# Both output projections of each layer as three products of rounded parts, with their weights split by ScalarE and GpSimd

## The reference, cut to what matters

```python
h = h + hybrid_mixer(rmsnorm(h, norm_mix[i]), ...)   # ends in concatenate([o_a, o_b, o_c, o_d]) @ w_out
h = h + cross_attn(rmsnorm(h, norm_xa[i]), mem, ...) # ends in o @ wo
h = h + swiglu(...)       # layer 0;  moe_swiglu(...) with 8 experts, top 2, in layer 1
```

## Time and profile before

| | us |
|---|---|
| median of 3 runs | 1512.05 (1511.49 to 1512.98) |
| the profiled execution | 1512.51 |
| its span in the trace | 1510.7 |
| PE busy | 1450.5 |
| DVE busy | 1086.0 |
| ACT busy | 914.1 |
| POOL busy | 51.8 |

### The profile page before, as it was taken

One profiled execution on the slowest core, in us unless ns is written; L12 is line 12 of the kernel. 1 busy time (PEld: TensorE's weight loads), 2 busy tenths in 40 slices (PEclk: granted clock), 3 DMA queues, 4 the chain that ended last, 5 costly groups with the idle time before them and its releaser, 6 DMA issues.

```text
span 1510.7 us, 19223 instructions
## 1 busy us (share of the span) xinstructions
PE 1450.5 (96%) x7312; PEld 1143.1 (76%) x7312; DVE 1086.0 (72%) x1116; ACT 914.1 (61%) x965; POOL 51.8 (3%) x64
## 2 busy tenths in 40 slices
PE   7999999999999999999999999999999999899997
PEld 5776679999877666788888777777777677677675
DVE  1615255555452526988798799899899898998996
ACT  2222243344322224777777688788887797887885
POOL 0230000000014000000000000000000000000000
PEclk9999999999999999999999999999999999999999
DMA  9522523542553055799899899999999999999991
GB/s 320 182 104 77 203 82 128 208 168 85 189 202 109 29 203 201 261 366 371 305 367 365 332 399 415 409 415 413 412 416 410 415 417 406 419 417 407 413 419 59
DMA packets 120581, 435.04 MB, mean 288 GB/s; under 512 B 5694, under 2 KB 30420, under 8 KB 113364
## 3 DMA queue, kind: packets, MB, share of 16 engines
q1 hardware_dynamic: 120340, 433.83, 74.6%
q0 software_dynamic: 192, 0.53, 0.1%
HBM read 433.28 MB, written 1.05 MB: 288 GB/s over the span
## 4 chain that ended last, share of the span: by engine, by line
PE 66%; DVE 17%; issue 12%; ACT 4%; DMA 0%; SPq 0%; DVEq 0%; ACTq 0%
PE bank L1902 23%; PE bank L1474 12%; DVE ring_lo L1380 12%; PE bank L1451 8%; PE bank L1456 6%; PE bank L1736 4%; PE bank L1928 3%; ACT w_hi L865 2%; PE bank L1848 2%; PE bank L1910 1%; DVE h L1217 1%; PE bank L1440 1%; PE bank L1778 1%; PE bank L1631 1%; PE bank L1430 1%
## 5 line engine op out<-in xcount | busy, mean ns | idle before, releaser
L1380 DVE TENSOR_TENSOR ring_lo<-ring,w_hi 128x2048 fp32r<-128x2048 f32 (+1 forms) x352 | 731.7, 2121 | 74.2 <-ACT w_hi L865 73.5
L865 ACT ACTIVATE w_hi<-ring 128x2048 fp32r<-128x2048 f32 (+1 forms) x352 | 610.3, 1777 | 138.1 <-PE bank L1902 138.0
L1902 PE MATMUL bank<-w_hi,xg 128*128 128x512 f32 x1120 | 408.5, 395 | 5.2 <-DVE ring_lo L1380 4.0
L1902 PE MATMUL bank<-ring_lo,xg 128*128 128x512 f32 x896 | 360.3, 402 | 19.4 <-DVE ring_lo L1380 17.3
L1902 PEld LDWEIGHTS bank<-w_hi,xg 128*128 128x128 f32 x1120 | 211.5, 189 | 51.1 <-DVE ring_lo L1380 4.4
L1902 PEld LDWEIGHTS bank<-ring_lo,xg 128*128 128x128 f32 x896 | 168.4, 188 | 76.1 <-DVE ring_lo L1380 41.6
L1902 PE MATMUL bank<-ring_lo,at_hi 128*128 128x512 f32 x400 | 162.3, 406 | 5.0 <-DVE at_hi L1363 5.0
L1902 PE MATMUL bank<-w_hi,at_hi 128*128 128x512 f32 x400 | 157.5, 394 | 0.5 <-DVE at_lo L1365 0.5
L1160 DVE TENSOR_TENSOR wf_lo<-ring,wf_hi 128x1024 fp32r<-128x1024 f32 x66 | 80.6, 1223 | 60.0 <-ACT wf_hi L743 60.0
L743 ACT ACTIVATE wf_hi<-ring 128x1024 fp32r<-128x1024 f32 x66 | 69.6, 1058 | 70.4 <-PE bank L1474 68.8
L1902 PEld LDWEIGHTS bank<-ring_lo,at_hi 128*128 128x128 f32 x400 | 75.1, 188 | 41.6 <-DVE ring_lo L1380 22.2
(11 more groups left out here) (337 smaller groups left out, 1635.3 us busy)
## 6 DMA issues: line engine op xcount, KB each, us to landing
ring<-in_moe_w SPq DMA_DIRECT2D x168, 2048.0 KB, 11.6
ring<-in_ffn_w SPq DMA_DIRECT2D x18, 1536.0 KB, 6.7
ring<-in_w_in SPq DMA_DIRECT2D x6, 2048.0 KB, 15.2
ring<-in_w_out SPq DMA_DIRECT2D x8, 1024.0 KB, 5.0
ring<-in_ffn_w SPq DMA_DIRECT2D x3, 2048.0 KB, 7.8
ring<-in_w_in SPq DMA_DIRECT2D x4, 1024.0 KB, 15.0
ring<-in_xa_wkv SPq DMA_DIRECT2D x2, 2048.0 KB, 14.8
ring<-in_w_in SPq DMA_DIRECT2D x2, 1184.0 KB, 7.3
```

Of the source, the lines that this page charges most:

```text
L865: act.activation(w_hi[:, i % NB, 0:cols.stop - cols.start], ring[:, slot_of(u), cols], ACT.Copy)\
L1380: dve.tensor_tensor(ring_lo[slot_of(u)][:, cols], ring[:, slot_of(u), cols], w_hi[:, i % NB, 0:cols.stop - cols.start], sub).then_inc(S["l ...
L1902: ins = mm(dst[:, :], st_, mv, start=opens, stop=closes, skip_group_check=small)
```

## The change

Both output projections become three products of rounded parts each. Their slots hold 2048 elements in a half of a slot of 4096, so the other half is free.

- ACT rounds the f32 weights of the slot into its upper half (`row_hi`), once for each of the five slots of a layer (`ROWS`: the four of `w_out`, and U_WO). These five instructions stand behind the copies kT, kdr, bu, uv0 and the copy of group 3.
- POOL writes the rest over the f32 weights in the lower half (`row_lo`), two before its wait for `bu`, three behind `pool_out`. It counts them up in `wkv_scaled`, six a layer with the scaling of U_WKV.
- DVE splits the activations: y is first scaled into `pw1`, then rounded to `mix_hi` and its rest put in `mix_lo`; groups 0, 2 (rows 0:2, 4:6) and the output of the cross-attention get a copy and a subtraction each, group 3 (rounded by ACT) a subtraction. `mix_hi` has the place of `mixT`, `mix_lo` the upper half of slot U_WQ.
- PE runs `times_rows`, with 12 products a token tile and group, and waits for POOL's count before each.

The diff, without the lines that only rename:

```diff
+        mix_hi = nc.alloc_sbuf_tensor_at("mix_hi", [P, KT, SEQ], F32R, offset=base, align_bytes=32)
+        mix_lo = ring_lo[U_WQ][:, 2048:4096].rearrange("p (k c) -> p k c", k=KT)
+        xo_hi, xo_lo = mix_hi[:, 0:2, :], mix_hi[:, 2:4, :]
...
+        ROWS = tuple(U_WOUT + n for n in range(4)) + (U_WO,)
...
+            return ring_lo[ROWS[n]][:, 2048:4096]
...
+            return ring_lo[ROWS[n]][:, 0:2048]
...
                 i.then_inc(S["wkv_scaled"], 1)
 
+                def rows_split(n):
+
+                    gp.wait_ge(S["bias_row"], hi_of_rows(layer, n))
+                    gp.tensor_tensor(row_lo(n), ring[:, ROWS[n], 0:2048], row_hi(n), ALU.subtract)\
+                      .then_inc(S["wkv_scaled"], 1)
+                for n in range(2):
+                    rows_split(n)
                 gp.wait_ge(g_ev["bu"], L1)
...
                 gp.wait_ge(S["pool_out"], L1)
+                for n in range(2, len(ROWS)):
+                    rows_split(n)
...
+                def rows_split(n):
+
+                    act.wait_ge(arrived[ROWS[n]], (layer * (16 * LAYER_TURNS) + 32))
+                    act.activation(row_hi(n), ring[:, ROWS[n], 0:2048], ACT.Copy).then_inc(S["bias_row"], 1)
                 out_of("k", kT[:, :, :], v3(ps[4], 0, 512, 2))
+                rows_split(0)
                 act.wait_ge(S["kd_ps"], L1)
                 act.activation(kdr, v3(ps[2], 0, 256, 2), ACT.Copy).then_inc(S["kdr_done"], 1)
+                rows_split(1)
                 out_of("bu", bu[:, :, PAD:PAD + SEQ], v3(ps[6], 0, 512, 2))
+                rows_split(2)
                 out_of("uv0", uvg[:, 0, :], ps[7][:, :], ACT.Gelu_apprx_tanh)
+                rows_split(3)
                 out_of("uv1", uvg[:, 1, :], ps[4][:, :], ACT.Gelu_apprx_tanh)
...
+                act.activation(mix_hi[:, 6:8, :], v3(ps[7], 0, 512, 2), ACT.Copy).then_inc(S["mt_a"], 1)
+                rows_split(4)
...
-                    i = dve.tensor_scalar(mixT[:, 2 + m, :], ps[5][:, 256 * m:256 * m + 256],
+                    i = dve.tensor_scalar(pw1[:, m, PAD:PAD + SEQ], ps[5][:, 256 * m:256 * m + 256],
                                           pcol[:, R_PB + m:R_PB + m + 1], pcol[:, R_PS + m:R_PS + m + 1], add, mult)
-                i.then_inc(g_ev["y"], 1)
+                link(i)
+                link(dve.tensor_copy(mix_hi[:, 2:4, :], pw1[:, :, PAD:PAD + SEQ]))
+                dve.tensor_tensor(mix_lo[:, 2:4, :], pw1[:, :, PAD:PAD + SEQ], mix_hi[:, 2:4, :], sub)\
+                   .then_inc(g_ev["y"], 1)
...
-                dve.tensor_copy(mixT[:, 0:2, :], v3(ps[4], 0, 512, 2)).then_inc(S["mt_v"], 1)
+                link(dve.tensor_copy(mix_hi[:, 0:2, :], v3(ps[4], 0, 512, 2)))
+                dve.tensor_tensor(mix_lo[:, 0:2, :], v3(ps[4], 0, 512, 2), mix_hi[:, 0:2, :], sub).then_inc(S["mt_v"], 1)
+                dve.wait_ge(S["mt_a"], L1)
+                dve.tensor_tensor(mix_lo[:, 6:8, :], v3(ps[7], 0, 512, 2), mix_hi[:, 6:8, :], sub).then_inc(S["mt_v"], 1)
                 dve.wait_ge(S["mto_ps"], L1)
-                dve.tensor_copy(mixT[:, 4:6, :], v3(ps[5], 0, 512, 2)).then_inc(S["mt_v"], 1)
+                link(dve.tensor_copy(mix_hi[:, 4:6, :], v3(ps[5], 0, 512, 2)))
+                dve.tensor_tensor(mix_lo[:, 4:6, :], v3(ps[5], 0, 512, 2), mix_hi[:, 4:6, :], sub).then_inc(S["mt_v"], 1)
...
-                dve.tensor_copy(oxT[:, :, :], v3(ps[1], 0, 512, 2)).then_inc(S["xo_done"], 1)
+                link(dve.tensor_copy(xo_hi, v3(ps[1], 0, 512, 2)))
+                dve.tensor_tensor(xo_lo, v3(ps[1], 0, 512, 2), xo_hi, sub).then_inc(S["xo_done"], 1)
...
+                def times_rows(bank, xh, xl, n, opens, closes):
+
+                    pe.wait_ge(S["wkv_scaled"], lo_of_rows(layer, n))
+                    wh, wl = v3(row_hi(n), 0, 2048, 2), v3(row_lo(n), 0, 2048, 2)
+                    for half in range(2):
+                        cs = slice(512 * half, 512 * half + 512)
+                        for k in range(2):
+                            for x, y in ((xh, wh), (xh, wl), (xl, wh)):
+                                i = mm(ps[bank + half][:, :], x[:, k, :], y[:, k, cs],
+                                       start=opens and k == 0 and x is xh and y is wh,
+                                       stop=closes and k == 1 and x is xl)
+                    return i
```

More of the change, by code:

```diff
@@ L201, in build @@
         base = nc.sbuf_base
+        assert base % 32 == 0
         xnT = sb("xnT", [P, KT, SEQ])
-        mixT = xnT
+        mix_hi = nc.alloc_sbuf_tensor_at("mix_hi", [P, KT, SEQ], F32R, offset=base, align_bytes=32)
+        mix_lo = ring_lo[U_WQ][:, 2048:4096].rearrange("p (k c) -> p k c", k=KT)
+        xo_hi, xo_lo = mix_hi[:, 0:2, :], mix_hi[:, 2:4, :]
         qidx = sb("qidx", [P, 1024])
@@ L322, in build @@
         vn = uvg[:, :, 256:512]
-        oxT = kT
         f_sil = v3(uvg[:, 1, :], 0, 512, 2)
@@ L407, in ffn_buf, with row_hi, row_lo, hi_of_rows @@
             return bufs[:, (i + NB - FFN_EARLY) % NB, :]
+        ROWS = tuple(U_WOUT + n for n in range(4)) + (U_WO,)
+        def row_hi(n):
+            return ring_lo[ROWS[n]][:, 2048:4096]
+        def row_lo(n):
+            return ring_lo[ROWS[n]][:, 0:2048]
+        def hi_of_rows(layer, n):
+            return 1 + len(ROWS) * layer + (n + 1)
+        def lo_of_rows(layer, n):
+            return (len(ROWS) + 1) * layer + (n + 2)
         def as_piece(w, buf):
@@ L716, in _ @@
                 act.wait_ge(S["mt_ps"], L1)
-                act.activation(mixT[:, 6:8, :], v3(ps[7], 0, 512, 2), ACT.Copy).then_inc(S["mt_a"], 1)
+                act.activation(mix_hi[:, 6:8, :], v3(ps[7], 0, 512, 2), ACT.Copy).then_inc(S["mt_a"], 1)
+                rows_split(4)
                 norm(1, R_XA)
@@ L1647, in _ @@
                 pe.wait_ge(arrived[U_WKV], landed[1])
-                pe.wait_ge(S["wkv_scaled"], L1)
+                pe.wait_ge(S["wkv_scaled"], lo_of_rows(layer, 0) - 1)
                 pe.wait_ge(g_ev["uv0"], L1)
@@ L1724, in _ @@
                         transpose_rows(5, oc).then_inc(S["mto_ps"], 1)
-                        pe.wait_ge(S["mt_v"], first)
+                        pe.wait_ge(S["mt_v"], 3 * layer + 1)
                     elif m == 3:
-                        pe.wait_ge(S["mt_a"], L1)
+                        pe.wait_ge(S["mt_v"], 3 * layer + 2)
                     else:
-                        pe.wait_ge(S["mt_v"], second)
+                        pe.wait_ge(S["mt_v"], 3 * layer + 3)
                     s = U_WOUT + i4
                     pe.wait_ge(arrived[s], landed[1])
-                    w = v3(ring[:, s, :], 0, 2048, 2)
                     for t in range(TT):
[L1734 to L1738, removed]
+                        i = times_rows(2 * t, mix_hi[:, 2 * m:2 * m + 2, P * t:P * t + P],
+                                       mix_lo[:, 2 * m:2 * m + 2, P * t:P * t + P], i4, i4 == 0, i4 == 3)
                         if i4 == 3 and t == 0:
@@ L1773, in _ @@
                 pe.wait_ge(arrived[U_WO], landed[1])
-                w = v3(ring[:, U_WO, :], 0, 2048, 2)
                 for t in range(TT):
[L1776 to L1779, removed]
+                    i = times_rows(4 + 2 * t, xo_hi[:, :, P * t:P * t + P], xo_lo[:, :, P * t:P * t + P], 4, True, True)
                     if t == 0:
```

## The result

| | us |
|---|---|
| before, median of 6 | 1511.88 (1510.96 to 1514.05) |
| changed, median of 6 | 1517.83 (1516.69 to 1518.67) |
| ratio | 1.0038, 95% interval 1.0028 to 1.0048 |
| profiled execution of the changed kernel | 1516.69, span 1514.9 |

The change makes the kernel 5.9 us slower, where 4 us less were forecast; the time lies outside the range. (The lines of `kernel.py` move: L1736 and L1778 are now L1774, L1045 is L1084, L912 is L951, L1071 is L1110, L1456 is L1503, POOL's subtraction is L588.)

The account below looks back on a forecast made before the run. PE, busy 96% of the span, was taken as the bound, its chain running through the two projections. Gains of 6.85 less 1.65 for splits and 3.1 for DVE's hold left 2.1 us a layer: 1508.3, about 1508.0 as median, range 1500.9 to 1511.5.

Parts of the forecast that it names:

- PE's new idle times: PE's added waits from the change, 1 to 3 us, were to leave its granted clock as it was.
- The row it rested on: Trace row cited for the unchanged clock: a stretch of 12 us with PE busy for 6.77 had 1.00.
- Products: Both output projections as three rounded products at 0.231 us each: 5.35 and 1.5 less, together 6.85 us a layer.
- Group y 1.0: Before the output projection, DVE's copy and subtraction for the first group delay PE's start: cost 1.0 us.
- xo 0.65: Before the cross-attention's projection, DVE's subtraction and its wait come on top: cost 0.65 us.
- ScalarE's roundings: Five roundings of 1.93 us on ACT, placed before waits of 4.97 to 8.24 us: cost nothing.
- GpSimd's subtraction 4.2: POOL's subtraction of 128x2048 takes 4.2 us, ends 3.0 and 6.2, four times the row at 128x512 being 4.16.
- The hold: POOL's third and fourth subtractions block DVE's bias_and_choice and small tensor_scalar: DVE 4.5 us late, 3.1 reaching the projection's start.
- Rival 1: DVE's small tensor_scalar is hardly held, lateness stays within the slack of 1.43 us, 5.2 a layer stands: 1501.9; chance 0.28.
- Rival 2: POOL's subtraction takes 6.2 us, DVE is 9.6 late, net 3.0 lost a layer: 1518; chance 0.08.
- point of decision: Threshold for a slower kernel: a loss of 5.2 us, DVE 6.6 late, a POOL instruction of about 5.2.
- Rival 3: Projections' products stay above 0.231 us, nothing gained at 0.287: 1512 to 1518; chance 0.04.

Follow-up runs that it names:

- the filled kernel: Changed kernel with six products of zero use added on PE where it waits, around the second tile's attention; 1511.0 us, ratio to before 0.9987.
- three ways of avoiding them: Changed kernel with GpSimd's subtractions moved away from DVE's SBUF work (1505.3 us), without the small tensor_scalar (1503.7), or with each subtraction cut into four (1504.7).
- the moved kernel: Changed kernel with ScalarE's roundings earlier, three of GpSimd's subtractions before bu's pooling and two behind group y; 1505.3 us, ratio 0.9956.
- the scalars from SBUF: Changed kernel with the small tensor_scalar of the gated MLP's variance taking its two scalars from SBUF, not as immediates; 1519.0 us, ratio 1.0045.
- the splits alone: Kernel before plus only ScalarE's five roundings and GpSimd's five subtractions a layer, projections still f32 products; 1527.9 us, ratio 1.0109.
- DVE late by itself: Kernel before with four reductions of 1.22 us put into DVE's queue behind bias_and_choice, DVE 5.0 us late; 1527.4 us, ratio 1.0101.
- quartered: Changed kernel with each of GpSimd's subtractions cut into four of 128x512; 1504.7 us, ratio 0.9955.

## Why the prediction was wrong

**The step that failed** is the last sentence of its sum: "PE's new idle times, 1 to 3 us, leave the clock as it is". The waits came as forecast, 1.1 and 1.7 us, and behind them the clock fell to 1.2 GHz and cost 4.85 us in layer 0 and 2.77 in layer 1. Filling the waits gave it back, and DVE's lateness alone, with nothing of the change, brought it about again (1527.4 us).

The row it rested on was read wrongly. The earlier trace rows shows 1.00 over 12 us with PE busy for 6.77, but it ends at 608.0, and PE came back from a wait of 3.99 us at 607.72. The next stretch of the same kernel, and its first product:

```profile
608.00:610.00 2.00, 2.00 (x6) 1.54 (x6) 2.00 (x4) 0.00 (x0) 0.00 (x0) 0.50 0.00 0
```

```profile
607.72 0.57 PE L1902 MATMUL bank<-w_hi,xg 128*128 128x512 f32 x1 [3.99 <-DVE ring_lo L1380]
```

The kernel before shows the fall; it stands in the records of the products behind a wait, not in the stretch of the wait. Had the row been taken 2 us further, a fall behind PE's waits would have been a rival.

**The other steps, in their order.**
- Products: the pace was put at 0.231 us and is 0.233 (16.79 / 72), with 0.244 in cross-attention's 24. 27.98 us with the transposes became 22.92, 7.07 became 5.86: 6.3 instead of 6.85.
- Group y 1.0: measured 1.00 (35.24 - 34.24). xo 0.65: from the projection's end to the next one's start it was 29.54 (165.62 to 195.16) and is 30.18 (168.22 to 198.40), 0.64.
- ScalarE's roundings cost nothing: right, 1.91 us each, and ACT still waits at all four places.
- GpSimd's subtraction 4.2 (3.0 to 6.2): 4.51. The Trainium skill's figure for 2048 f32 elements (GPSIMD Engine Reference, section 3.1), 4.5 us, was nearer than four times the row at 512.
- The hold: the two instructions named, 2.3 and 3.5 us forecast, took 2.58 and 3.69. The Trainium skill's rule on the shared port (SBUF — State Buffer, Who interferes with whom) agrees with these rows, and so does its exemption of instructions with one SBUF input (0.43 and 0.18 for the statistics). 3.1 us were to go through; the filled kernel shows 3.3.
- Rival 1 fell with its condition: the small instruction of two elements is held. Rival 2 fell too, its POOL time of 6.2 being 4.5; but its point of decision, DVE 6.6 us late, was wrong by the clock: 4.9 was enough. That its 1518 lies next to the measured 1517.8 is luck. Rival 3 fell.

With these sizes and no fall of the clock the sum is 3.3 + 1.0 + 0.64 - 6.3 = -1.3 a layer, 1509 us: inside the range, and hardly a gain. The clock's 7.6 make it +5.0; 5.9 were measured. So even without the clock the forecast 2.1 a layer was 1.3, by the products' term and the hold.

Of the gain of two f32 projections in three products, then, 12.5 us came; 3.3 go for the activations' split, 6.6 for DVE's lateness and 7.6 for the clock. The last two are avoidable, and three ways of avoiding them give 1503.7 to 1505.3 us, faster than either kernel and not told apart from each other.

## What to carry to other kernels

Work given to an idle GpSimd can be paid where VectorE next wants a second SBUF operand or a small SBUF-to-SBUF tensor_scalar: look in the timeline for what VectorE does in the microseconds it will run, and cut it up or move it. A microsecond of lateness ahead of TensorE is worth more than a microsecond once it opens waits: 2.5 us cost 1.2 a layer here, 5.0 cost 9.1. Read the clock behind a wait, in the products that follow it, never in the stretch that holds the wait.

## What the runs showed of the hardware

- An instruction of two elements (0.17 us) can be held for most of a GpSimd instruction, here 3.5 us of 4.5, with its scalars as immediates or in SBUF.
- The order between them: a DVE instruction that waits gets in before GpSimd's next when it waited first (the fourth subtraction took 5.49 us instead of 4.51, a quarter 2.25 instead of 1.27). In the moved kernel the second of two DVE instructions came 0.03 us behind the first and was held again, for the whole of the next subtraction (4.63 us).
- The lower clock lasted some 7 or some 14 us behind the same waits (128 to 142 us in layer 0 of the changed kernel, 510.4 to 517.2 in its layer 1), and with the scalars from SBUF it was the other way round between the layers. It cost 2.8 us in both layers with the splits alone, 4.9 and 2.8 in the changed kernel, 5.5 and 5.6 with DVE late by itself.
- The same products, from one kernel to the next, can meet the lower clock or not: at the start of layer 1 it lasted 3.4 us before, 6.8 with the splits alone, and was absent in three profiled executions (moved, quartered, DVE 5.0 us late).
